# Staggering VectorE and ScalarE by slots in the gated feed-forward, weights of its output projection split inside the loop's tail, and the first slot after a joint accumulated in other PSUM banks

## What is computed

```python
def rmsnorm(x, gain):
    x32 = x.astype(jnp.float32)
    y = x32 * lax.rsqrt(jnp.mean(x32 * x32, axis=-1, keepdims=True) + RMS_EPS)
    return (y * gain.astype(jnp.float32)).astype(x.dtype)

def conv_glu_ffn(xn, w_up, conv_w, conv_b, w_down):
    gu = xn @ w_up
    gate, up = jnp.split(gu, 2, axis=-1)
    gate = causal_dwconv(gate, conv_w) + conv_b.astype(gate.dtype)
    return (jax.nn.silu(gate) * up) @ w_down
...
        x = x + rmsnorm(h, norm_mix_post[l])
        h = memory_cross_attention(rmsnorm(x, norm_cross_pre[l]), rmsnorm(mem, mem_norm[l]), w_cq[l], ...)
        x = x + rmsnorm(h, norm_cross_post[l])
        h = conv_glu_ffn(rmsnorm(x, norm_ffn_pre[l]), w_ffn_in[l], ffn_conv_w[l], ffn_conv_b[l], w_ffn_out[l])
        x = x + rmsnorm(h, norm_ffn_post[l])
```

## Time and profile before

| what | us |
|---|---|
| median of 3 runs | 1574.51 (1574.4 to 1575.26) |
| the profiled execution's own time | 1577.13 |
| its span | 1575.2 |
| TensorE products, busy | 1489.5 |
| VectorE, busy | 1178.8 |
| ScalarE, busy | 839.6 |
| GpSimd, busy | 20.0 |
| mean granted TensorE clock | 0.98 of full |

### The profile page before, as it was taken

How to read it: one execution, slowest core, us unless ns; L and a number is a source line. 1 busy time by engine, 2 the same in 40 slices (tenths; PEclk the granted TensorE clock), 3 DMA queues, 4 the chain that set the end, 5 groups by cost and what they waited for, 6 DMA issues and landing times.

```text
span 1575.2 us, 29640 instructions
## 1 busy us (share of the span) xinstructions
PE 1489.5 (95%) x9912; PEld 1359.7 (86%) x9912; DVE 1178.8 (75%) x2246; ACT 839.6 (53%) x1205; POOL 20.0 (1%) x25
## 2 busy tenths in 40 slices
PE   7999978888798999999999999999999999999998
PEld 6889867888688988878999998999988888889997
DVE  4767666787646765866489999999888888876665
ACT  7635565434436366655667666667633334344443
POOL 0000000000002100000000000000000000000000
PEclk9999999999899999999999999999999999999999
DMA  7452433544453552245476676444477777756553
GB/s 270 146 183 81 161 108 107 161 156 153 149 185 107 188 161 81 86 155 187 150 229 222 214 229 206 135 138 145 160 236 244 236 246 239 244 201 203 187 188 142
DMA packets 97492, 276.37 MB, mean 175 GB/s; under 512 B 10760, under 2 KB 37256, under 8 KB 96908
## 3 DMA queue, kind: packets, MB, share of 16 engines
q1 hardware_dynamic: 65664, 240.54, 47.2%
q10 hardware_dynamic: 31756, 34.88, 6.4%
HBM read 260.16 MB, written 16.26 MB: 175 GB/s over the span
## 4 chain that ended last, share of the span: by engine, by line
PE 79%; DVE 11%; ACT 6%; issue 3%; DMA 1%; ACTq 0%; DVEq 0%; PEldq 0%
PE acc L1239 7%; PE acc L1242 7%; PE acc L1243 7%; PE acc L1161 5%; PE acc L1165 5%; PE acc L1166 5%; DVE sb_halves L1884 4%; PE acc L563 4%; PE ring L563 4%; PE ring L1203 4%; PE ring L566 4%; PE ring L567 4%; PE acc L567 4%; PE acc L566 4%; ACT sb_halves L1322 2%
## 5 line engine op out<-in xcount | busy, mean ns | idle before, releaser
L1884 DVE TENSOR_TENSOR sb_halves<-sb_raw,sb_halves 128x1024 fp32r<-128x1024 f32 x450 | 545.5, 1227 | 176.1 <-ACT sb_halves L1322 172.9
L1322 ACT ACTIVATE sb_halves<-sb_raw 128x1024 fp32r<-128x1024 f32 x450 | 471.3, 1060 | 357.1 <-PE acc L1239 167.0
L1161 PE MATMUL acc<-sb_XH,sb_halves 128*128 128x256 f32 x800 | 232.9, 291 | 3.9 <-ACT sb_early L1666 3.8
L1166 PE MATMUL acc<-sb_XH,sb_halves 128*128 128x256 f32 x800 | 226.1, 283 | 0.0
L1165 PE MATMUL acc<-sb_XL,sb_halves 128*128 128x256 f32 x800 | 226.1, 283 | 0.0
L1239 PE MATMUL acc<-sb_halves,sb_coefh 128*128 128x512 f32 x512 | 200.1, 391 | 2.0 <-DVE sb_coefl L2510 2.0
L1242 PE MATMUL acc<-sb_halves,sb_coefh 128*128 128x512 f32 x512 | 200.2, 391 | 0.0
L1243 PE MATMUL acc<-sb_halves,sb_coefl 128*128 128x512 f32 x512 | 199.9, 390 | 0.0
L563 PE MATMUL ring<-sb_XH,sb_halves 128*128 128x256 f32 x640 | 183.7, 287 | 14.9 <-DVE sb_halves L1884 14.8
L566 PE MATMUL ring<-sb_XL,sb_halves 128*128 128x256 f32 x640 | 181.0, 283 | 0.0
L567 PE MATMUL ring<-sb_XH,sb_halves 128*128 128x256 f32 x640 | 180.9, 283 | 0.0
(11 more groups left out here) (380 smaller groups left out, 2674.5 us busy)
## 6 DMA issues: line engine op xcount, KB each, us to landing
sb_raw<-wstream SPq DMA_DIRECT2D x450, 512.0 KB, 3.5
ahead<-sb_early ACTq DMA_DIRECT2D x100, 128.0 KB, 2.2
sb_area<-ahead ACTq DMA_DIRECT2D x98, 128.0 KB, 3.2
sb_area<-gains ACTq DMA_DIRECT2D x4, 512.0 KB, 4.3
sb_area<-consts SPq DMA_DIRECT2D x1, 1782.0 KB, 13.7
sb_area<-mem ACTq DMA_DIRECT2D x1, 1024.0 KB, 11.7
relvec<-relrow ACTq DMA_DIRECT2D x1, 1024.0 KB
sb_area<-keys ACTq DMA_DIRECT2D x1, 1024.0 KB, 7.1
```

Of the source, the lines that this page charges most:

```text
L1161: ins = mm(o, w[0], XH[:, c, :], start=c == 0, stop=False)
L1166: ins = mm(o, w[1], XH[:, c, :], start=False, stop=c == KC - 1)
L1322: A(hi[:, r, :], raw[:, r, :], ACT.Copy).then_inc(S("hi_ready"), 1)
L1884: tt(lo[:, r, :], raw[:, r, :], hi[:, r, :].bitcast(F32), ALU.subtract).then_inc(S("lo_ready"), 1)
```

## The change

In the feed-forward's loop, the first tap with the bias goes from VectorE to ScalarE, as an Identity activation with a scale and a bias for each partition. VectorE's round f now begins with the gate of chunk f - 1, then feeds, then waits for `ff_first` and makes the other two taps. ScalarE applies silu one round later (chunk f - 2 in round f) and rounds to `hidh` one round later (chunk f - 3). Both engines feed the third to sixth pieces of `down` inside the loop, in its rounds 22 and 23. `proj_unscaled` writes to `acc[:, 0, 0]` and `acc[:, 0, 1]`, has no job in the ring any more, and signals `first_done`; its readers wait on that. The roots go through `acc[:, 1, 0]`.

```diff
@@ proj_unscaled (TensorE)
-                banks = [bank(name)[:, 0:T], bank((*name, 1))[:, 0:T]]
+                banks = [acc[:, 0, j, 0:T] for j in range(2)]
...
-                    done(ins, (*name, 1) if j else name)
+                    ins.then_inc(S("first_done"), 1)
@@ root_row (TensorE)
-                    ins = nc.tensor.transpose(acc[:, 0, 0, t * P:(t + 1) * P], root_rows[:, t, :], ident)
+                    ins = nc.tensor.transpose(acc[:, 1, 0, t * P:(t + 1) * P], root_rows[:, t, :], ident)
@@ ScalarE
+            def first_copy(k, j, dst):
+
+                act.wait_ge(S("first_done"), 2 * (k - 2) + j + 1)
+                link(A(dst, acc[:, 0, j, 0:T], ACT.Copy), f"first_copied{k}")
...
-            for f in range(1, FC + 2):
+            for f in range(1, FC + 3):
                 if f < FC:
                     feed(("up", f))
+                elif f < FC + 2:
+                    feed(("down", f - FC))
                 if f <= FC:
-                    act.wait_ge(S("ff_conv"), f)
-                    g = (f - 1) % 2
-                    link(A(fa[:, g, :], fa[:, g, :], ACT.Silu), "ff_silu")
-                if f >= 2:
-                    act.wait_ge(S("ff_prod"), f - 1)
-                    link(A(hidh[:, f - 2, :], ht[:, f % 2, :], ACT.Copy), "ff_hid")
+                    g = f - 1
+                    act.wait_ge(S("ff_gate"), f)
+                    if f >= 3:
+                        act.wait_ge(S("ff_prod"), f - 2)
+                    link(A(fa[:, g % 2, :], gpad[:, g % 2, 0:256], ACT.Identity, scale=C("fconv", g), bias=C("fb", g)), "ff_first")
+                if 2 <= f <= FC + 1:
+                    act.wait_ge(S("ff_conv"), f - 1)
+                    g = f - 2
+                    link(A(fa[:, g % 2, :], fa[:, g % 2, :], ACT.Silu), "ff_silu")
+                if f >= 3:
+                    g = f - 3
+                    act.wait_ge(S("ff_prod"), g + 1)
+                    link(A(hidh[:, g, :], ht[:, g % 2, :], ACT.Copy), "ff_hid")
             root_ready()
-            for i in range(FC // 2 - 1):
+            for i in range(2, FC // 2 - 1):
                 feed(("down", i))
@@ VectorE
+            def gate_scaled(g):
+
+                if g:
+                    b = got(dve, ("up", g))
+                else:
+                    dve.wait_ge(S("first_done"), 3)
+                    b = acc[:, 0, 0, :]
+                link(tt(gpad[:, g % 2, 2:258], b[:, 0:T], root_T, ALU.mult), "ff_gate")
+
+            gate_scaled(0)
             for f in range(1, FC + 3):
-                if 1 < f < FC:
+                if 2 <= f <= FC:
+                    gate_scaled(f - 1)
+                if 2 <= f < FC:
                     feed(("up", f))
+                elif FC <= f < FC + 2:
+                    feed(("down", f - FC))
                 if f <= FC:
                     g = f - 1
                     o, p = fa[:, g % 2, :], gpad[:, g % 2, :]
-                    link(tt(p[:, 2:258], got(dve, ("up", g))[:, 0:T], root_T, ALU.mult), "dve_step" if g else "ffn_gate")
-                    link(ts(o, p[:, 0:256], C("fconv", g), C("fb", g), ALU.mult, ALU.add))
+                    dve.wait_ge(S("ff_first"), f)
                     link(stt(out=o, in0=p[:, 1:257], scalar=C("fconv", 22 + g), in1=o, op0=ALU.mult, op1=ALU.add))
...
-            for i in range(FC // 2 - 1):
+            for i in range(2, FC // 2 - 1):
                 feed(("down", i))
```

More of the change, by code:

```diff
@@ L237, in jobs @@
     norm(3, 1)
[L238 to L241, removed]
+    for f in range(1, FC):
         job(("up", f), "ffn_up")
@@ L268, in jobs @@
     norm(5, 1)
-    for i in range(8):
+    for i in range(1, 8):
         job(("pq", i), "pq_copied")
-        if i == 0:
-            job(("pq", 0, 1), "pq_copied")
     for t in range(NT):
@@ L1025, in _ @@
                 if i == 0:
-                    proj_unscaled(("T2", i), key, 4)
+                    proj_unscaled(key, 4)
                 else:
@@ L1542, in _ @@
                 x_root(2, t)
-            copy_job(("cq", 0), cqT[:, 0, :], "cq_copied")
-            copy_job(("cq", 0, 1), cqT[:, 1, :], "cq_copied")
+            for j in range(2):
+                first_copy(2, j, cqT[:, j, :])
             feed(("cq", 1))
@@ L1641, in _ @@
                     act.dma_start(xkeep, x.rearrange("p t d -> p (t d)")).then_inc(S("x_out"), 16)
-                    copy_job(("pq", 0), pqT[:, 0, :], "pq_copied")
-                    copy_job(("pq", 0, 1), pqT[:, 1, :], "pq_copied")
+                    for j in range(2):
+                        first_copy(5, j, pqT[:, j, :])
                 else:
@@ L1858, in turned_roots @@
                 dve.wait_ge(S("root_turned"), k - 2)
-                link(V.tensor_copy(root_T, acc[:, 0, 0, 0:T]), "root_copied")
+                link(V.tensor_copy(root_T, acc[:, 1, 0, 0:T]), "root_copied")
             def rest_turned(name, c, sem):
@@ L2217, in _ @@
                     dve.wait_ge(S("ff_silu"), g + 1)
-                    b = got(dve, ("up", g) if g else ("up", 0, 1))
-                    link(tt(ht[:, g % 2, :], fa[:, g % 2, :], b[:, T:2 * T] if g else b[:, 0:T], ALU.mult), "ffn_up")
+                    if g:
+                        b = got(dve, ("up", g))[:, T:2 * T]
+                    else:
+                        dve.wait_ge(S("first_done"), 4)
+                        b = acc[:, 0, 1, 0:T]
+                    link(tt(ht[:, g % 2, :], fa[:, g % 2, :], b, ALU.mult), "ffn_up" if g else "first_copied3")
                     link(tt(ht[:, g % 2, :], ht[:, g % 2, :], root_T, ALU.mult), "ff_prod")
@@ L2243, in column_scaled @@
                     for k in range(2):
-                        b = got(dve, ("T2", 0) if k == 0 else ("T2", 0, 1))
-                        tt(foxh[0:HD, 0, 0, 0, :] if k == 0 else foxh[0:HD, 0, 1, 0, :], b[0:HD, 0:T], root_T[0:HD], ALU.mult)
-                        link(tt(foxh[HD:P, 0, k, 1, :], b[HD:P, 0:T], root_T[HD:P], ALU.mult), "t2_copied")
+                        dve.wait_ge(S("first_done"), 5 + k)
+                        b = acc[:, 0, k, 0:T]
+                        tt(foxh[0:HD, 0, k, 0, :], b[0:HD], root_T[0:HD], ALU.mult)
+                        link(tt(foxh[HD:P, 0, k, 1, :], b[HD:P], root_T[HD:P], ALU.mult), "first_copied4")
                     return
```

26 lines of the change are left out of this document (13 added, 13 removed).

## The result

| | before | changed |
|---|---|---|
| median of the runs | 1574.52 us (1574.4 to 1575.26, 4 runs) | 1531.18 us (1527.9 to 1536.53, 4 runs) |
| profiled execution, span | 1577.13, 1575.2 us | 1536.53, 1534.6 us |
| granted clock, mean over the span | 0.981 | 0.986 |

The ratio is 0.9727 [0.9698, 0.9756]: 43.3 us less, where 43.7 were forecast (1531). The changed kernel's executions are further apart than those of before were, and these four go with their mean clock: 1536.5 us at 0.986, 1532.2 at 0.990, 1530.2 at 0.991, 1527.9 at 0.994.

A forecast was written before the change was run, and what follows sets the result against it. TensorE, busy 1489.5 of 1575.2 us, was taken as the bound, with only its gaps and low clock to win. Gains of 19.6 + 10.1 + 14.0 = 43.7 us from 1574.5 gave 1530.8, say 1531; range 1524 to 1541.

The forecast's parts named there:

- The loop, 19.6 us: Feed-forward loop: 20 slots go from 6.74 to 5.76 us each, TensorE setting the pace; gain 19.6 us.
- The step that named the cause: Feed-forward loop: VectorE and ScalarE wait for each other in a ring, 1.25 us of VectorE's 6.81 us round idle.
- The tail, 10.1 us: Start of `down`: feeding pieces inside the loop removes a 7.4 us gap and 2.7 us of low clock; gain 10.1 us.
- the whole 7.4 us: TensorE's gap before the third piece of `down`, from 410.07 to 417.47, forecast to go.
- tail unchanged, 1541: Rival at `down`: ScalarE is held in round 22, so the 7.4 us gap moves instead of going; 1541 us, chance 0.06.
- The joints, 14.0 us: First slot behind each of four joints: TensorE starts earlier without waiting for the ring's bank; 4 x 3.5 us, between 8 and 17.
- The three cases of the prediction: Gain at joint 2: 2.0 us if the clock stays low 6.6 us, 3.5 if it returns sooner, 4.2 at best.
- TensorE starts about 204.7: Joint 2: first product behind the transposes starts at about 204.7 instead of 207.41, 2.7 us earlier.
- a few microseconds for stretches of low clock elsewhere: Outside loop, tail and joints: allowance in the 1524 to 1541 range for low clock beginning and ending at other moments.
- The rival of a slower kernel: Rival in the loop: busy engines make the chip lower the clock, 115 us lost over 20 slots; 1580 to 1645, chance 0.04.
- its part 3: First slot behind a joint: the prediction's section on these slots, counting 0.213 us per product at low clock.
- The estimate of 5.2 us for 48 products: Loop slot by the skill page's 109 ns gap: 10 us more to win; the prediction kept the measured 5.76 us.

The follow-up runs named there:

- experiment 8: Changed kernel with first tap and gate back in their old places on VectorE; silu and hidden-chunk rounding still a round later: 1531.66 us, ratio 0.9713.
- experiment 4: Changed kernel with the down pieces from the third on fed behind the loop, as before the change: 1537.95 us, ratio 0.9772.
- second profile: Profile of the changed kernel, unaltered, run once more in later rounds: median 1527.14 us, ratio 0.9684.
- Experiment 1: Changed kernel without the accumulator banks, so the first slot behind a joint stays in the ring, loop and tail as changed: 1547.48 us, ratio 0.9826.
- experiment 3: Changed kernel with the first tap and bias back on VectorE and no Identity on ScalarE: 1531.02 us, ratio 0.972.
- experiment 7: Changed kernel with five unread fp32 products ahead of the second tile's transposes at joints 2 to 4: 1526.26 us, ratio 0.9691.
- experiment 9: Changed kernel without the accumulator banks, plus five unread products ahead of the second tile's transposes at joints 2 to 4: 1545.28 us, ratio 0.9801.
- experiment 10: Changed kernel with five unread products at joints 2 to 4, run again beside the unaltered changed kernel: 1526.93 us, ratio 0.9688.

## Why the prediction was right, step by step

**The loop, 19.6 us: 19.5 measured.** The third slot starts at 264.39 and `down` at 379.67. VectorE's round was costed at 5.15 us and is 5.11 without its idle 0.65; ScalarE's slack in front of the taps at 1.2 us and is 1.1. The Identity was put at silu's 0.42 us and takes 0.58 to 0.60: its scale and its bias are each a column with one value for each partition, which silu and the copy here don't have, and the difference was hidden. That the columns cost it was not tried. The step that named the cause was right, and experiment 8 makes it sharper: it is the round's delay of silu and of the hidden chunk. What the prediction didn't see is that the tap could have stayed: the VectorE sum with it, 5.15 + 0.45 = 5.60, was also under 5.76, and its own rows gave that.

**The tail, 10.1 us: 10.5 measured.** From the first product of `down` to the transposes of joint 4's second tile it was 74.8 us and is 64.3. The third piece's remainder ends 1.9 us after the start of `down` (VectorE's timeline of the changed kernel, two remainders from 380.39), those of the fifth and sixth at 6.6 and 8.3, where 1.9, 6.5 and 8.1 were counted:

```profile
380.39 2.36 DVE L1893 TENSOR_TENSOR sb_halves<-sb_raw,sb_halves 128x1024 fp32r<-128x1024 f32 x2
...
385.08 1.23 DVE L1893 TENSOR_TENSOR sb_halves<-sb_raw,sb_halves 128x1024 fp32r<-128x1024 f32 x1
386.74 1.23 DVE L1893 TENSOR_TENSOR sb_halves<-sb_raw,sb_halves 128x1024 fp32r<-128x1024 f32 x1 [0.44 <-ACT sb_halves L1322]
```

The sum was right and its attribution wrong: the whole 7.4 us, and the low clock behind it, was given to the feeding in the loop, which is worth 5.5 us of the 10.5. The rest belongs to the staggered loop (experiment 4), so the rival "tail unchanged, 1541" stood too high; by experiment 4 it would have been 1538.

**The joints, 14.0 us: 13.8 measured in the profiled executions.** Windows from the start of the second tile's transposes to the first product of the slot behind, joints 2 to 5, before:

```profile
203.22:215.29 12.07, 9.13 (x57) 8.71 (x57) 8.97 (x23) 8.01 (x20) 0.00 (x0) 0.72 0.49 154
252.21:263.74 11.53, 9.03 (x56) 8.45 (x57) 9.14 (x24) 8.29 (x20) 0.00 (x0) 0.70 0.46 156
479.25:491.51 12.26, 9.32 (x56) 8.90 (x57) 9.65 (x23) 8.19 (x20) 8.79 (x10) 0.72 0.38 120
721.30:733.70 12.40, 9.36 (x56) 8.95 (x57) 9.07 (x23) 8.54 (x23) 0.00 (x0) 0.72 0.44 148
```

and of the changed kernel:

```profile
203.67:213.09 9.42, 9.42 (x56) 9.29 (x57) 8.95 (x23) 7.98 (x20) 0.00 (x0) 0.68 0.34 124
249.99:258.49 8.50, 8.34 (x56) 8.13 (x57) 8.26 (x21) 8.17 (x20) 0.00 (x0) 0.80 0.35 123
443.94:452.44 8.50, 8.34 (x56) 8.13 (x57) 7.88 (x20) 8.20 (x20) 5.14 (x8) 0.80 0.17 62
682.15:690.19 8.04, 7.23 (x56) 6.62 (x57) 7.75 (x20) 7.94 (x22) 0.00 (x0) 1.00 0.25 85
```

Gains of 2.7, 3.0, 3.8 and 4.4. The three cases of the prediction were 2.0, 3.5 and 4.2, by what the clock does, and these four lie between and about them. What limits a joint at full clock is what the prediction named: the last group of `XL` products waits for VectorE's `XL` (0.35 us at joint 5, 0.36 at joint 2 in the second profile). At joint 2 in that profile the gain is 4.05 us; the best case was 4.2. "TensorE starts about 204.7" came out as 205.3 in the first profile and 204.56 in the second, at low and at full clock. The prediction let the clock come back 4.4 us behind the transposes; it took 6.1, 4.1 and 4.7 us at joints 2 to 4. In the second profile the four joints take 32.6 us and not 34.5, a gain of 15.7, so that 13.8 came so close to 14.0 is in part luck.

How much of such a gain is the pause and how much the clock? Experiment 1 keeps the ring, and in its profile joint 5 has the pause of 2.9 us and no low clock:

```profile
697.20:707.01 9.81, 6.78 (x56) 6.36 (x57) 9.05 (x23) 8.53 (x23) 0.00 (x0) 1.00 0.31 93
```

9.8 us against 8.04: the pause itself costs 1.8 us. The other 2.6 of joint 5's 4.4 us are low clock, of which the changed kernel has none at joint 5 in either of its profiles.

**The sum.** 19.5 + 10.5 + 13.8 = 43.8, and the spans differ by 40.6. Of the missing 3.2 us low clock outside the three places explains about 2, by this estimate: while TensorE works, it has 17.0 us of it there before and 23.8 in the changed kernel's first profile. It costs 0.45 us ahead of joint 2 and about 1.8 in the experts' stage. The other 1.1 us are in the experts' first projection, here from the slot behind joint 5's to the first product of the next step, before and in the changed kernel:

```profile
733.70:773.10 39.40, 38.71 (x341) 38.52 (x339) 23.56 (x18) 20.58 (x23) 0.00 (x0) 1.00 0.60 201
```

```profile
690.19:730.67 40.48, 39.75 (x341) 39.57 (x339) 24.93 (x22) 21.18 (x25) 0.00 (x0) 1.00 0.66 223
```

The clock is 1.00 and the products are the same, but many of them start 0.118 us apart where they started 0.113 before. Why is open; in the second profile the stretch takes 39.23 us. The prediction allowed "a few microseconds for stretches of low clock elsewhere" in its range and not in its sum. So the time of 1531.18 met the forecast of 1531 by chance in its last microseconds: the second set of runs gave 1527.14, 48.4 us below the kernel before in the same rounds (1575.55), with less low clock (mean clock 0.992 to 0.995).

**The rival of a slower kernel** needed low clock in the loop. In every loop with no gap (both profiles of the changed kernel, experiments 1, 3, 4 and 7 to 10) the clock is 1.00 from the third slot to the end of the loop. The prediction also priced this rival too high: it took 11.5 us for a slot at 1.2 GHz, while its own 0.213 us for a product (its part 3) gives 10.2, so 90 us more in 20 slots and not 115. The estimate of 5.2 us for 48 products, from the Trainium skill, page "TensorE: Matmul & The Clock Gate", section "Back-to-back issue gap", which gives its formula for an isolated product, didn't come true: with the waits gone, the products of 256 columns in the loop still start 0.12 us apart.

## What to carry to other kernels

When two helper engines take turns inside a round and the engine they feed waits at the end, add up each one's own work first. If each sum is below the slot, the waits are the cost; here it was enough to let one engine work on the result of the round before. Moving work from the busier helper to the other can make it worse, because it adds a link: 7.06 us a round against 6.81. Low clock costs little where the engine would soon wait anyway: 3.4 us of it cost 0.5 us at a joint. And before a few microseconds are credited to an edit, run the unedited kernel beside it in the same rounds: here the medians of one unchanged kernel on two occasions were 4 us apart.

## What the runs showed of the hardware that was not expected

- The same kernel with the same pauses has low clock at different places from one execution to the next. Joint 2 of the changed kernel had 0.58 over 8 us once and 1.00 once. The profiled executions had 41.4 and 21.0 us of low clock within spans of 1534.6 and 1527.0 us, in stretches of 3 to 7 us, and the times of the nine executions are up to 0.7% apart (1525.1 to 1536.5 us). What decides where it falls was not settled.
- Five unread products in place of a 2.2 us part of a pause kept the clock up at all three joints in both profiles, but the time gained was within the spread. Low clock costs a joint only 0.5 to 1.4 us, and in the second profile a low stretch of 10 us came in the first block's mixer (142 to 153 us).
- An Identity with a scale and a bias for each partition on 128 x 256 takes 0.58 to 0.60 us on ScalarE, where silu and a copy of the same size take 0.42.
- The same stream of products of 256 columns, at a granted clock of 1.00, took 40.5, 39.4 and 39.2 us in three profiles (341 products behind joint 5). Not explained.
- ScalarE's table load, 1.28 us, can stand between the last hidden chunk and the next rounding of a weight piece; in the changed kernel, behind the feeding of four pieces, no wait of TensorE follows it in `down`.
